# A decoder step on one core: the first steps of the compression in another order, position bias as two more columns of an operand, gates and key turns moved into the projections

## The reference, cut to what matters

```python
def _nsa_compress(kv, w1, pos, w2):                       # kv: (B, L, 2, heads, 64)
    n_sub = L // 16; nc = n_sub - 1
    sub = kv[:, :n_sub * 16].reshape(Bsz, n_sub, 16, 2, 2, 64)
    w1r = w1.reshape(2, 2, 16, 64, 64)
    proj = jnp.einsum('bnpshd,srpde->bnshre', sub, w1r)
    bias = jnp.einsum('sf,sfe->se', pos.reshape(2, -1), w1)   # the position bias
    h = bias[None, None, :, None, :]
    for r in range(2):
        h = h + proj[:, r:r + nc, :, :, r]
    out = jnp.einsum('bnshe,sef->bnshf', gelu(h), w2)
    return out[:, :, 0], out[:, :, 1]
```

## Time and profile before

| | |
|---|---|
| time, median of 3 runs | 1845.7 us (1844.94 to 1845.77) |
| the profiled execution | 1835.2 us, of which the span is 1833.4 us |
| PE busy | 94% of the span |
| DVE, ACT, POOL busy | 43%, 29%, 18% |
| granted clock of TensorE, mean | 0.976 of 2.4 GHz |

### The profile page before, as it was taken

One profiled execution on the slowest core, in us unless ns is written; L12 is line 12 of the kernel. 1 busy time (PEld: TensorE's weight loads), 2 busy tenths in 40 slices (PEclk: granted clock), 3 DMA queues, 4 the chain that ended last, 5 costly groups with the idle time before them and its releaser, 6 DMA issues. The chain is left out here.

```text
span 1833.4 us, 26633 instructions
## 1 busy us (share of the span) xinstructions
PE 1722.8 (94%) x10063; PEld 1148.6 (63%) x10063; DVE 794.4 (43%) x1929; ACT 523.8 (29%) x1248; POOL 337.2 (18%) x352
## 2 busy tenths in 40 slices
PE   8999999999999989899888999999998998999986
PEld 6687777877877868788666765575444444444432
DVE  1154664664664410265888653472222222222216
ACT  2224234234233220365676543111111111111110
POOL 0011210211211120131554551001111111111100
PEclk9999999999999989799799999999999999999999
DMA  8071221221232252152100564978999999999988
GB/s 244 1 227 45 71 73 49 66 78 49 60 84 48 47 166 55 48 176 84 36 2 1 181 219 153 359 324 340 375 420 420 419 421 420 419 420 420 419 349 321
DMA packets 168543, 371.70 MB, mean 203 GB/s; under 512 B 36903, under 2 KB 114719, under 8 KB 143584
## 3 DMA queue, kind: packets, MB, share of 16 engines
q1 hardware_dynamic: 148208, 308.69, 45.7%
q0 software_dynamic: 19728, 60.06, 9.2%
q10 hardware_dynamic: 480, 1.25, 0.2%
HBM read 337.75 MB, written 48.15 MB: 210 GB/s over the span
## 5 line engine op out<-in xcount | busy, mean ns | idle before, releaser
L861 PE MATMUL bank<-xT,arena 128*128 128x272 f32 x1440 | 368.2, 399 | 0.0
L861 PEld LDWEIGHTS bank<-xT,arena 128*128 128x128 f32 x1440 | 259.8, 190 | 62.3 <-issue 16.3
L2874 PE MATMUL bank<-arena,kvt 128*64 128x512 f32 (+1 forms) x816 | 256.1, 610 | 21.6 <-issue 20.7
L2874 PEld LDWEIGHTS bank<-arena,kvt 128*64 128x64 f32 (+1 forms) x816 | 88.1, 148 | 151.5 <-issue 151.5
L2971 PE MATMUL bank<-arena,kvt 128*64 128x512 f32 (+1 forms) x408 | 127.8, 598 | 2.2 <-issue 2.1
L3297 DVE SCALAR_TENSOR_TENSOR kvt<-kvt,arena,bank 128x256 f32<-128x256 f32 x37 | 17.8, 481 | 239.0 <-ACT kvt L3079 239.0
L1291 POOL TENSOR_TENSOR arena<-arena 128x512 f32<-128x512 f32 x40 | 46.3, 1157 | 381.5 <-DVE arena L1382 257.0
L2874 PE MATMUL bank<-xT,kvt 128*64 128x512 f32 (+1 forms) x208 | 97.0, 622 | 9.3 <-issue 9.3
L2711 POOL DMA_INDIRECT hT<-x_rows,rows_i x37 | 37.5, 1014 | 350.9 <-DVE rows_i L3232 328.9
L3079 ACT ACTIVATE kvt<-bank 128x256 f32<-128x256 f32 x37 | 14.2, 383 | 276.9 <-PE bank L2874 276.9
L1657 PE MATMUL bank<-xT,arena 128*128 128x272 f32 x352 | 83.4, 401 | 8.6 <-PEq L168 8.6
(11 more groups left out here) (519 smaller groups left out, 2960.3 us busy)
## 6 DMA issues: line engine op xcount, KB each, us to landing
arena<-in_w_exp_gate SPq DMA_DIRECT2D x51, 1024.0 KB, 22.5
arena<-in_w_exp_up SPq DMA_DIRECT2D x51, 1024.0 KB, 25.5
arena<-in_w_exp_down SPq DMA_DIRECT2D x51, 1024.0 KB, 23.8
arena<-in_w_in SPq DMA_DIRECT2D x48, 512.0 KB, 5.5
kvt<-in_w_exp_down SPq DMA_DIRECT2D x13, 1024.0 KB, 23.1
xT<-in_w_exp_gate SPq DMA_DIRECT2D x13, 1024.0 KB, 21.6
xT<-in_w_exp_up SPq DMA_DIRECT2D x13, 1024.0 KB, 25.0
y_rows<-arena SPq DMA_DIRECT2D x1, 12800.0 KB, 39.9
```

The costliest lines, as they stand in the source:

```text
L861: last = mm(banks[2 * (i % 2) + half][:, 0:HALF], wh[blk % RING][:, k, :], xT[:, k, half * HALF:(half + 1) * HALF], start=(k == 0), stop=( ...
L2874: last = mm(banks[2 + 4 * (t % 2)][cols, :], xgT[:, k, cols], ewgu[i % EBUF][:, :, k], start=(k == 0), stop=(k == KD - 1))
```

## The change

- The bank pair of projection block n is now that of parity n+1, so that block 10 is in banks 2 and 3, and quads 0 are turned into banks 0 and 1 without waiting for its save. PE waits for that save before page 0.
- The key turns (now `keys_turned`) come after projection block 8; ACT saves them between the saves of blocks 9 and 10.
- ACT's save of a merge gate block applies the tanh itself, two instructions of 272 columns in place of a copy; the separate pass is gone. DVE scales each block after its save. The tanh of `gt` is now ACT's first work in the block.
- The position rows are written by ACT as columns 64 and 65 of the prompt's operand `Xp`, and the prompt's first layer is 66 columns wide, in bank 5 instead of bank 4. The 32 one-column matmuls, `posT` and their copy are gone. The bias is now the sum of the earlier half of column 64 and the later half of column 65, by a copy on ACT and an addition on DVE.
- PE's order is: quads 0, page 0, the position rows, page 1, the prompt's first layer for s = 0, page 2, the same for s = 1, page 3, batch 0. The prompt's second layer comes behind batch 0's first layer, its gelu on ACT after the second of the four saves in batch 0, and its results are saved at batch 0's end.

```diff
-                        last = mm(banks[2 * (n % 2) + half][:, 0:HALF], wh[blk % RING][:, k, :],
+                        last = mm(banks[2 * ((n + 1) % 2) + half][:, 0:HALF], wh[blk % RING][:, k, :],
                                   xT[:, k, half * HALF:(half + 1) * HALF], start=(k == 0), stop=(k == KD - 1))
                 last.then_inc(prj_banked, 1)
-            pe.wait_ge(prj_saved, ATT_BLOCKS)
-            for br in range(2):
-                for t in range(4):
-                    last = tr(banks[6 + br][:, t * P:t * P + P], kvt[:, t, (br + 1) * 256:(br + 1) * 256 + P], ident[:, :])
-                last.then_inc(kt_banked, 1)
-            pe.wait_ge(c2_in, 16 * 3)
-            tr(banks[4][:, 0:32], pos_rows[0:32, :], ident[0:32, 0:32]).then_inc(posr_banked, 1)
+                if n == ATT_BLOCKS - 3:
+                    keys_turned()
+            pe.wait_ge(prj_saved, ATT_BLOCKS - 1)
...
             turn_quads(0, page_p)
+            pe.wait_ge(prj_saved, ATT_BLOCKS)
             turn_page(0)
+            pe.wait_ge(c2_in, 16 * 3)
+            tr(banks[4][:, 0:32], pos_rows[0:32, :], ident[0:32, 0:32]).then_inc(posr_banked, 1)
+            turn_page(1)
+            pe.wait_ge(w1_in, 16 * 4)
             pe.wait_ge(posr_saved, 1)
-            pe.wait_ge(w1_in, 16 * 4)
-            for s in range(2):
-                for m in range(16):
-                    last = mm(banks[5][0:HD, s:s + 1], Wx[:, s, m % 8, m // 8 * HD:m // 8 * HD + HD], posT[:, s, m:m + 1],
-                              start=(m == 0), stop=(m == 15))
-            last.then_inc(posr_banked, 1)
-            pe.wait_ge(pg_saved_a, 1)
-            pe.wait_ge(pg_saved_v, 1)
             for s in range(2):
                 for j0 in (0, 4):
-                    last = first_layer(banks[4][:, s * 64:s * 64 + 64], Xp, s, j0)
+                    last = first_layer(banks[5][:, s * P:s * P + 66], Xp, s, j0)
+                if s == 0:
+                    turn_page(2)
             last.then_inc(hid_banked, 1)
-            for n in range(1, 4):
-                turn_page(n)
-            pe.wait_ge(gelu_done, 1)
-            ... (the prompt's second layer)
+            turn_page(3)
             for b in range(NB):
...
                 last.then_inc(hid_banked, 1)
-                if b >= 1:
+                if b == 0:
+                    prompt_second()
+                else:
                     second_layer(b - 1)
...
+            actv(gt[:, 0:4], kvt[:, 0:4, 768:816], ACT.Tanh, scale=0.5)
...
-                    last = actv(dst[...], banks[2 * (n % 2) + half][:, 0:HALF], ACT.Copy)
+                    last = actv(dst[...], banks[2 * ((n + 1) % 2) + half][:, 0:HALF],
+                                ACT.Tanh if merge_gate else ACT.Copy, scale=0.5 if merge_gate else 1.0)
...
-            actv(mgB, mgB, ACT.Tanh, scale=0.5)
...
+            save_quads(0)
             sc.wait_ge(posr_banked, 1)
-            actv(posT, banks[4][:, 0:32].rearrange("p (s n) -> p s n", s=2), ACT.Copy).then_inc(posr_saved, 1)
+            actv(Xp[:, :, :, 64:66].rearrange("p s j r -> p s r j"), banks[4][:, 0:32].rearrange("p (s r j) -> p s r j", s=2, r=2),
+                 ACT.Copy).then_inc(posr_saved, 1)
+            for i in range(1, 5):
+                save_quads(i)
...
                     for n in range(4):
                         save_quads(4 * (b + 1) + 1 + n)
+                        if b == 0 and n == 1:
+                            prompt_hidden()
...
-            step(V.tensor_scalar(mgB, mgB, 1.0, 0.5, ALU.add, ALU.mult))
...
+            for m in range(8):
+                dve.wait_ge(prj_saved, len(NQ_AHEAD) + m + 1)
+                step(V.tensor_scalar(mgB[:, m], mgB[:, m], 1.0, 0.5, ALU.add, ALU.mult))
+            for i in range(5):
+                save_quads(i)
             dve.wait_ge(half_saved, 1)
+            early = banks[5][0:HD, 0:256].rearrange("p (s m n) -> p s m n", s=2, n=32)
+            step(V.tensor_tensor(cbias[0:HD], cbias[0:HD], early[:, :, 2, 0], ALU.add))
```

99 lines of the change are left out of this document (48 added, 51 removed).

## The result

| | before | after |
|---|---|---|
| time, median of 4 runs | 1845.56 us (1844.94 to 1845.77) | 1829.24 us (1824.03 to 1830.46) |
| the profiled execution | 1835.2 us | 1829.45 us, of which the span is 1827.6 us |
| granted clock of TensorE, mean | 0.976 | 0.975 |

The ratio is 0.9907, with a 95% interval of 0.9891 to 0.9924: the changed kernel is faster by 16.3 us. The rival "full clock throughout" had said 1830.3.

A forecast was written before the change was run, and what follows sets the result against it. PE's waits and half-clock work between the projections and batch 1 were taken as the bound. 15.7 - 0.3 - 2.3 = 13.1 us won, so 1845.7 - 13.1 = 1832.6 us, range 1829.5 to 1839.5.

The forecast's parts named there:

- full clock throughout: Rival: the denser order keeps TensorE at 2.4 GHz; gain 15.4 us, time 1830.3; chance 0.16.
- Steps 1 to 6: PE's line from last projection to batch 1's first turn, rebuilt at full clock: batch 1 at 774.1, 15.7 us won.
- ACT late in batch 0: Table load and gelu between ACT's saves in batch 0 delay the third and fourth, costing batch 1 0.3 us.
- One such fall: One fall of the clock at the gap ahead of batch 0 slows its first step, costing 2.3 us.
- third fall of the clock: The fall after the 2.3 us gap ahead of batch 0, expected to stay with a gap of 2.0 us.
- Half clock through the first steps: Rival: the DMA wait drops the clock, the half-width first layer holds it down; gain 7.1 us, 1838.6; chance 0.21.
- The attention's clock gives back 4 to 8: Rival: lower clock in the attention behind the compression returns 4 to 8 us, time 1836 to 1841; chance 0.09.
- Taking over the difference of 10.5 us between profile and median: Whole kernel: the profiled-to-median difference stays, so 1822.1 us profiled and 1832.6 as the time.

The follow-up runs named there:

- e2_after_again: The changed kernel run again with no edit; 1817.83 us beside 1836.59 for before, ratio 0.9899.
- e1_before_again: The kernel before run again with no edit; 1836.11 us beside 1836.59 for before, ratio 0.9998.
- e5_projection_part_only: The kernel before with only key turns, tanh and scaling moved within the projections; 1832.85 us beside 1836.57 for before, ratio 0.9981.
- e4_without_projection_part: The changed kernel with key turns, tanh and scaling put back after the projections, old banks; 1831.16 us beside 1836.59 for before, ratio 0.9964.
- e11_small_loads_early: The changed kernel with position rows and second-layer weights loaded ahead of the last projection weights; 1819.66 us beside 1836.59 for before, ratio 0.9910.
- e12_best: The changed kernel with the small loads early and page 3 turned ahead of the first layer's second half; 1818.84 us, ratio to before 0.9906.
- e14_attention_later_by_1_3: The changed kernel with an ACT copy of 1400 columns ahead of the compression's last save; 1823.31 us beside 1837.08 for before, ratio 0.9918.
- e15_attention_later_by_2_5: The changed kernel with an ACT copy of 2800 columns ahead of the compression's last save; 1823.41 us beside 1837.08 for before, ratio 0.9924.
- e6_projection_and_positions: The kernel before with the work moved within the projections and the position columns, old order of steps; 1828.11 us, ratio to before 0.9962.
- e7: The kernel before with the prompt's first layer streaming its 64 columns twice; 1833.72 us beside 1836.57 for before, ratio 0.9991.
- e3: The kernel before with only the positions as two columns, no one-column matmuls; 1835.32 us beside 1836.59 for before, ratio 0.9990.
- e13_after_third: The changed kernel with no edit, on a further chip; 1819.70 us beside 1837.08 for before, ratio 0.9899.
- e10: The changed kernel with both halves of the prompt's first layer ahead of pages 2 and 3; 1823.38 us beside 1836.59 for before, ratio 0.9924.
- e9: The changed kernel with an ACT copy of 3264 columns ahead of the last save before batch 0; 1827.59 us, ratio to before 0.9955.

## Why the prediction was off by 3.4 us

**Steps 1 to 6, the sum at full clock: right, to 0.2 us.** 15.7 forecast, 15.7 measured (15.7 again in e2_after_again against e1_before_again); from the third block, without the projections' start, 15.5, 15.7 and 15.6. Step by step, from the projections' start: no wait above 0.3 ahead of page 0; the wait for the small DMAs 1.35 for 1.3; the first layer 1.74 a half (754.56 to 756.30) for the 1.7 taken; batch 0 at 761.83, 1.9 us behind page 3, for 2.0; batch 0 11.37 for 11.4. The first layer at full clock, which no row of before showed, was taken as half of its half-clock time, and that held. The Trainium skill (TensorE: Matmul & The Clock Gate, "LDWEIGHTS (loading the stationary operand)") gives, by its formula, an estimate of 107 ns for a load of 128 columns. The 66-column records follow each other at 0.112 us at the full clock, so the trace is near it there, and at the half clock it is not: 0.213 us in e5_projection_part_only.

One reading of the rows behind the prediction was wrong without touching the sum: DVE and ACT are not both idle for over half of the two stretches. ACT is busy 16.12 of 26.53 us in the first and DVE 6.75 of 12.97 in the second.

**ACT late in batch 0, 0.3 us: the term failed.** ACT of the changed kernel in order of time (L2018 saves of quads, L2036 and L2038 the prompt's gelu), answering to the earlier trace rows:

```profile
767.10 1.28 ACT L2036 ACT_TABLE_LOAD   x1
...
768.56 0.67 ACT L2038 ACTIVATE arena<-arena 64x62 f32<-64x62 f32 x4
769.25 3.12 ACT L2018 ACTIVATE arena<-bank 64x256 f32<-64x256 f32 x8
```

The third save did start 1.2 us late (769.25; its turns were done at about 768.1) and the last ended at 772.37, less than 0.1 late. But PE was then in the prompt's second layer until 773.20. I had counted those 0.82 us on PE and not as cover for the same saves.

**"One such fall", 2.3 us: the step that failed.** I had said that the third fall of the clock stays, because the gap ahead of batch 0 stays ("a gap of 2.0 us"). The gap stayed, 1.87 us, and no fall came in any of the eight profiles with such a gap or a shorter one ahead of batch 0 (the changed kernel three times, e4_without_projection_part with 1.88, e11_small_loads_early, e12_best, e14_attention_later_by_1_3, e15_attention_later_by_2_5). The error is in how I read rows 4: I had cut a stretch at the gap, 774.40 to 776.70, found 0.52 there, and took the gap for its cause. Cut where the clock changes, the kernel before shows:

```profile
771.00:774.47 3.47, 2.26 (x18) 1.58 (x17) 3.33 (x9) 3.39 (x10) 2.46 (x3) 0.99 0.59 157
774.47:776.73 2.26, 0.00 (x0) 0.00 (x0) 1.41 (x6) 2.16 (x7) 0.09 (x1) 0.50 0.91 266
```

The clock went down when the gap began, so the gap can't be its whole cause. In the six profiles with the old order of steps and this gap the fall stands 0.1 us ahead of the gap's start (e1_before_again), 0.05 behind it (before), 0.2 (e6_projection_and_positions), 0.3 (e7), 0.55 (e3) and 0.7 (e5), while the changed kernel stays at full clock for all of its 1.87. What stands ahead in the old order are 3.47 us with 2.26 of work, in them the wait of 0.83 us for the gelu and the small matmuls of the second layer. The changed kernel has moved that group behind batch 0 and has five groups of turns and first layer without a wait there instead. Two things stay open. The old gap is also longer, 2.3 us for 1.87, and no run has a gap of 2.3 behind the new order, or one of 1.9 behind the old group; the moment of the fall alone speaks against its length. And the wait for the gelu and the small matmuls were not taken apart.

That the miss was no more than 0.3 us beyond the range is luck. Of the 15.7 us, 10.7 were given back behind the changed stretch in the profiles of the first set, and the median of before in that set stood at a level that no later set showed; the two nearly cancel in the timed 16.3.

**The rivals.** "Full clock throughout" (0.16) is what happened up to batch 1; its 0.3 for ACT was not lost either. "Half clock through the first steps" named a mechanism that is real and was shown in e4_without_projection_part, behind a wait of 6.13 us; behind a wait of 1.35 it doesn't start. "The attention's clock gives back 4 to 8" (0.09) happened as well, in the first profile: 5.2 us. In e2_after_again and e13_after_third it gained 2. So two cases that I had held apart came together, and the timed gain of the first set, 16.3, is not simply the 15.7.

**Taking over the difference of 10.5 us between profile and median: not borne out.** The changed kernel's profile and median agree (1829.45 and 1829.24), and so do those of before elsewhere (1836.98 and 1836.11 in e1_before_again). The profile of before, 1835.2, looks like the executions of the later sets and not like its own set's 1845.6. The profiled pair therefore differs by 5.8 us and the timed pair by 16.3, and neither is a clean account of the other. What made before 9 us slower in the first set, and the attention of the changed kernel 7 us slower there, stays open: no execution of before at 1845 us was traced, and no later set showed it. Like with like, e1_before_again against e2_after_again, the two spans differ by 20.3 us: 15.7 up to the compression's end (198.5 and 182.8 from the projections' start), 2.0 in the attention, and the rest behind it.

## What to carry to other kernels

- Before a fall of the clock is put down to a gap, cut the windows at the moment at which the clock changes, and look at what ran ahead of that moment.
- Waits and one-column matmuls on one path don't add up singly: here two parts were worth 0.6 and 0.5 alone and 10.1 together, because either cause alone kept the same later work at half clock. Take all of them away before judging one.
- A kernel that swings between the levels carries several us of difference from stage to stage with no edit at all (175.0 and 182.3 us for the same attention). A local gain is read from the stretch up to the next unchanged stage, in more than one execution, and from a starting point at which the clock is the same in all of them: here the first matmul of the block was 1 us too coarse.
- Compare windows that lie as far behind the same instruction in both kernels, and look first whether an inserted delay has moved what it was meant to move.

## What the runs showed of the hardware that was not expected

- Gaps of PE behind groups of turns: 1.87 or 1.88 us kept the clock in seven profiles; 2.77 (e10), 3.27 (e3), 4.61 (e9) and 6.13 (e4) lost it. It fell 3.4 us into the gap of 4.61, but 1.1 us behind the end of the one of 2.77: the row in which the clock is low need not hold the cause.
- PE busy without a break can lose the clock: 5.08 of 5.10 us of one-column matmuls brought it down within them, and 6.90 of 6.90 us of 64-column matmuls left it there. Twice the columns took 6.49 us for 7.09, and the half-clock stretch was 3.4 us shorter (6.8 for 10.2, e7).
- Behind loads of 128 columns, a matmul record of 64 or of 128 columns took the same 0.213 us at half clock (e5, e7), and one of 66 columns 0.112 at full (after).
- The same kernel in an identical order took 175.0, 175.0 and 182.3 us in its attention; the mean clock went 0.93, 0.93, 0.91 with it. And in the sixteen profiles the unchanged first projection matmuls ran at half clock for anything from 3.7 to 6.2 us.
